# Scores of the first two attention items moved in among the value projections, in two attentions of one long fp32 kernel

## The chip, the cores and the metric
One NeuronCore of a Trainium2 chip runs the whole program in one launch. The metric is the device time of one execution in microseconds. The engines are TensorE (PE in the profile; PEld is its weight load), VectorE (DVE), ScalarE (ACT), GpSimd (POOL) and SyncE (SP), which issues the weight DMAs.

## The reference
Two transformer stacks run one after the other on 256 tokens of width 1024 and a context of 256 tokens, all in fp32. The parts that matter are the attentions of layers 0 and 1 of the first stack, which both attend densely:

```
# gqa: 16 heads of 64, 4 key/value heads; queries of x and of the context
q, k, v = split(h @ w_in); q = rms_norm(q); k = rms_norm(k); rope on the x half
p = softmax(q @ k^T * 64**-0.5); out = p @ v
# mla: 16 heads, query and key of 64 + 32 (rope), value of 64; queries of x only
q = rms_norm(cq) @ w_uq; kv = rms_norm(ckv) @ w_ukv
p = softmax((qn @ kn^T + qr @ kr^T) * 96**-0.5); out = p @ v
```

Context queries see 256 keys, x queries all 512. Feed-forward layers, other mixers (RWKV, sparse attention) and a mixture of experts follow; the change does not touch them.

## The kernel before
Each engine has its own instruction stream, written out by hand in Python; the order in the source is the order in the queue of that engine. Engines meet through named events: `did(...)` counts a semaphore up, `wait_ge(*at(...))` waits for it. The eight PSUM banks are handed out in a fixed rotation by `take`, and a taker waits for the event that frees its bank.

Weights come in 1 MB chunks through a ring of four. A matmul in fp32r with split operands needs a high and a low part of each weight unit of 1024 columns: ACT copies the high part (`hi_units`, row `WHI<-ring`), DVE subtracts for the low part (`lo_units`, row `WLO<-ring,WHI`), and PE runs three matmuls for each tile (lines 77 to 79). Scores, rope products and value products are plain fp32 matmuls of line 74, transposes are line 82, and each of them shows as two instructions. Every ACT activation is recorded at line 85.

An attention (class `Attention`) is cut into items, each a pair of heads and one or two blocks of 128 queries. Item i passes through: `scores_pe` (PE, two banks), `max_dve` (two reductions of line 105 and a small scaling), `exp_act` (ACT), `normalise_dve` (reciprocal and scalings by the row sums), `turn_pe` (eight transposes), `copy` (one bank by DVE, one by ACT) and `values_pe`. The loops `attend_pe`, `attend_act` and `attend_dve` run them in a software pipeline. In step i PE issues the scores of item i+1, the transposes of item i-1 and the value products of item i-2. ACT issues the exponentials of item i and then the copy of item i-2. GQA has 24 items, MLA 16. GQA's item 0 has two query blocks of 256 keys, items 1 and 2 have one block of 512 keys; every MLA item has one block of 512.

Before the GQA attention, `gqa_pe` projects queries and keys and last the values: four blocks t4 of 128 tokens, 24 matmuls each, with sum and rope product of query group 7 behind block 0. DVE copies each block out (`gvt`), and behind block 0 it finishes the rope of group 7 and the query scale RQ (event `rq`). Two steps of an unrelated row product (`ada_part_pe` s = 6, 7) stand between the values and the attention.

Before the MLA attention, `mla_pe` projects eight groups of keys (`mk_up`, pr = 0..7, six matmuls of 512 columns each) and then the values, for half = 0, 1 and t4 = 0..3, six matmuls each. ACT copies each key group out in two activations of 64x512 (event `mk`, pr) between its weight splits. DVE copies the shared rope part of the keys into all heads, two copies for each pr, the last with event `mkrope`. The values are copied out by DVE.

`scores_pe` first waits for the list `ready`. For GQA this is the duplicated keys (`gkd`) and the finished query group of that pair. For MLA it is one list for all pairs: `("mk", 7)`, `("mkrope",)`, `("mqr", 3)`, `("mq", 7)`, that is, the copies of the last key group, of all rope parts, and of the queries.

Of the kernel before, what the change touches and what calls it, by code (L numbers as in the profile page):

```python
# [25 lines left out]
class Signals:  # L26
# [12 lines left out]
    def did(self, name, *events):  # L39
        self.n[name] = self.n.get(name, 0) + 1  # L40
        for ev in events:
            assert ev not in self.events, ev
            self.events[ev] = (name, self.n[name])
        return self.sem(name), 1
# [8 lines left out]
    def at(self, *ev):  # L53
        if self.known is None:
            return None, 1
        return self.known[ev]
# [491 lines left out]
def program(nc, ctx, known):  # L548
# [1093 lines left out]
    def gqa_rope_pe(pe, m):  # L1642
        b = take(pe, ("gr", m), ("gsin", m))
        pe.wait_ge(*at("gqn" if m >= 8 else "gqe", m))
        pe.wait_ge(*at("d_cr", "gqa"))
        pe.mm(b[:, 0:256], gperm, g_dst(m)[:, 256:512], True, True).then_inc(*did("group", ("grot", m)))

    def gqa_pe(pe):
        st, steps = L["gqa_in"], L["ada0"]
        def second_job(k):  # L1650
            for s in {1: (0, 1, 2), 2: (3,)}.get(k, ()):
                ada_part_pe(pe, L["ada_pe"][4 + s], 1, s)
            if k == 3:
                ada_turn_pe(pe, 1)
                give(bank_of["rs", 0])

        project_block(pe, st, [(("gq", m), ("gsq", m), 512, hx(0, 512)) for m in GQA_ORDER[:4]], normed(0), second_job)
        after = [[(gqa_sum_pe, 8), (gqa_sum_pe, 9), (gqa_sum_pe, 0), (gqa_sum_pe, 1), (gqa_rope_pe, 0), (gqa_rope_pe, 1)],
                 [(gqa_spread_pe, 8), (gqa_spread_pe, 9), (gqa_sum_pe, 2), (gqa_rope_pe, 2)],
                 [(gqa_rope_pe, 8), (gqa_rope_pe, 9), (gqa_sum_pe, 3), (gqa_rope_pe, 3)],  # L1660
                 [(gqa_sum_pe, 4), (gqa_rope_pe, 4)], [(ada_turn_pe, 2), (gqa_sum_pe, 5), (gqa_rope_pe, 5)],
                 [(gqa_sum_pe, 6), (gqa_rope_pe, 6)]]
        for t, m in enumerate(GQA_ORDER[4:]):
            ada_part_pe(pe, steps[t], 2 + t // 4, t % 4)
            project_group(pe, st, 4 + t, ("gq", m), ("gsq", m), 512, hx(0, 512), normed(0))
            if t == 0:
                sums["gk"] = take(pe, ("gksum",), ("gkroot",))
                sums["gq"] = take(pe, ("gqsum",), ("rqroot",))
                keep(bank_of["gqsum",])
            for f, arg in after[t]:  # L1670
                f(pe, arg)
        pieces = [p for [(_, _, p)] in st.groups[10]]
        for t4 in range(4):
            b = take(pe, ("gv", t4), ("gvt", t4))
            for k, p in enumerate(pieces):
                pe.wait_ge(*at("lo", p.unit))
                X = HHI[:, k, 128 * t4:128 * t4 + 128], HLO[:, k, 128 * t4:128 * t4 + 128]
                m = pe.mm3(b[:, 0:256], X, split_of(p), k == 0, k == 7)
                ev = closes(p) if t4 == 3 else ()
                if k == 7:  # L1680
                    ev = ev + (("gv", t4),)
                if ev:
                    m.then_inc(*did("group", *ev))
            if t4 == 0:
                gqa_sum_pe(pe, 7)
                give(bank_of["gqsum",])
                gqa_rope_pe(pe, 7)

    def gqa_act(a):
        def out(m):  # L1690
# [44 lines left out]
    def gqa_dve(v):  # L1735
        st = L["gqa_in"]
        ropes = [[], [0, 1], [2, 8], [9, 3], [4], [5], [6]]
        lo_units(v, st.ahead[0])
        for t in range(6):
            lo_units(v, st.ahead[4 + t])  # L1740
            for m in ropes[t]:
                gqa_rope_dve(v, m)
            if t == 0:
                v.wait_ge(*at("gkroot"))
                v.recip(GK, GK).then_inc(*did("recip", ("gkrt",)))
            if t == 1:
                for m in (8, 9):
                    v.wait_ge(*at("gks", m))
                    v.wait_ge(*at("gqe", m))
                    v.tt(g_dst(m), g_dst(m), bank("gks", m)[:, :], ALU.mult).then_inc(*did("qk", ("gqn", m)))  # L1750
            if t == 5:
                ada_job_dve(v, 2)
        lo_units(v, st.ahead[10])
        for m in ropes[6]:
            gqa_rope_dve(v, m)
        for t4 in range(4):
            v.wait_ge(*at("gv", t4))
            v.cp(gVT[:, t4, :], bank("gv", t4)[:, 0:256]).then_inc(*did("v_copy", ("gvt", t4)))
            if t4 == 0:
                gqa_rope_dve(v, 7)  # L1760
                v.wait_ge(*at("rqroot"))
                v.recip(RQ, RQ).then_inc(*did("qk"))
                v.wait_ge(*last("qk"))
                v.ts(RQ, RQ, 0.125, None, ALU.mult).then_inc(*did("qk", ("rq",)))

    GQA_ROPES = (0, 1, 2, 8, 9, 3, 4, 5, 6, 7)

# [16 lines left out]
        lambda pr: [("gkd",), ("gfin", pr)], [("gvt", 3)], lambda q, hd: RQ[:, q, hd])  # L1784

    def attend_pe(pe, A, step=None):
        A.scores_pe(pe, 0)
        for i in range(A.n + 2):
            if i + 1 < A.n:
                A.scores_pe(pe, i + 1)  # L1790
            if 1 <= i <= A.n:
                A.turn_pe(pe, i - 1)
            if i >= 2:
                A.values_pe(pe, i - 2)
            if step:
                step(i)
# [10 lines left out]
                step(i)  # L1807

    def attend_dve(v, A, step=None):
        for i in range(A.n + 2):  # L1810
            if i < A.n:
                A.max_dve(v, i)
            if 1 <= i <= A.n:
                A.normalise_dve(v, i - 1)
            if i >= 2:
                A.copy(v, i - 2, 0)
            if step:
                step(i)

# [50 lines left out]
    def mla_pe(pe):  # L1870
        st = L["mla_in"]
        lat = [(("mq_in", m), ("mcq", m), 256, hx(256, 256)) for m in range(3)]
        project_block(pe, st, lat + [(("mk_in", 0), ("mck", 0), 512, hx(0, 512))], normed(2))
        project_group(pe, st, 4, ("mk_in", 1), ("mck", 1), 512, hx(0, 512), normed(2))
        for k in range(3):
            sum_pe(pe, 3, k)
        project_group(pe, st, 5, ("mk_in", 2), ("mck", 2), 512, hx(0, 512), normed(2))
        spread_pe(pe, 3)
        mla_rope_pe(pe, "k", ("mck", 2))
        for k in range(2):  # L1880
            sum_pe(pe, 4, k)

        def of_parts(parts, low):
            return (lambda k: (parts[0][:, k, :], parts[1][:, k, :])), (lambda k: [(low, k)])

        X, needs = of_parts(CQP, "cql")
        for j in range(4):
            project_group(pe, st, 6 + j, ("mr_up", j), ("mqr_raw", j), 256, X, needs)
        spread_pe(pe, 4)
        for t in range(8):  # L1890
            project_group(pe, st, 10 + t, ("mq_up", t), ("mq", t), 256, X, needs)
            if 1 <= t < 5:
                mla_rope_pe(pe, t - 1, ("mqr_raw", t - 1))
        X, needs = of_parts(CKP, "ckl")
        for pr in range(8):
            project_group(pe, st, 18 + pr, ("mk_up", pr), ("mk", pr), 512, X, needs)
        for half in range(2):
            for t4 in range(4):
                b = take(pe, ("mv", half, t4), ("mv", half, t4))
                z = slice(128 * t4, 128 * t4 + 128)  # L1900
                for k, [(_, _, p)] in enumerate(st.groups[26 + half]):
                    pe.wait_ge(*at("lo", p.unit))
                    m = pe.mm3(b[:, :], (CKP[0][:, k, z], CKP[1][:, k, z]), split_of(p), k == 0, k == 1)
                    ev = closes(p) if t4 == 3 else ()
                    if k == 1:
                        ev = ev + (("mv_up", half, t4),)
                    if ev:
                        m.then_inc(*did("group", *ev))
# [42 lines left out]
    def mla_dve(v):  # L1951
# [41 lines left out]
        v.wait_ge(*at("mqr", 3))  # L1993
        for half in range(2):
            lo_units(v, st.ahead[26 + half])
            for t4 in range(4):
                v.wait_ge(*at("mv_up", half, t4))
                v.cp(mVT[:, t4, 512 * half:512 * half + 512], bank("mv", half, t4)[:, :]).then_inc(
                    *did("v_copy", ("mv", half, t4)))
# [1774 lines left out]
    def scalar(a):  # L3774
# [19 lines left out]
        gqa_act(a)  # L3794

        def ada_rows(i):
            if i in (0, 13, 21):
                ada_row_act(a, *{0: (3, 2), 13: (6, 3), 21: (7, 6)}[i])
            if i == 18:
                hi_units(a, L["gqa_out"].first)  # L3800
        attend_act(a, gqa, ada_rows)
# [216 lines left out]
```

## Time and profile before

| | us |
|---|---|
| runs | 2056.47, 2063.47, 2063.95 |
| median | 2063.47 |
| profiled execution, span from first to last instruction | 2057.3 |
| PE busy in it | 1936.8 (94%) |
| DVE, ACT busy | 1349.8 (66%), 1073.3 (52%) |
| mean granted PE clock, share of full | 0.969 |

For the profiled execution only the span is given, no time of its own beside it. The span lies 6.2 us under the median of the runs and 0.8 us above the lowest run. GQA's value projection begins at about 120 us of the span and MLA's at 757 us.

### The profile page before, as it was taken

The numbers are of one execution on the slowest core, as the hardware profiler recorded it, in microseconds if no ns is written. First come the engines' busy times: TensorE is split into PE (matmuls) and PEld (weight loads), VectorE is DVE, ScalarE is ACT, GpSimd is POOL, SyncE is SP. The second block draws the span as 40 slices with busy tenths as digits, with TensorE's granted clock in tenths as the row PEclk, the third lists the DMA queues.
The fourth block names the chain that finished last, engine by engine and source line by source line (L and its number), as shares of the span: only waits on it lengthen the run. The fifth ranks groups of instructions, "written<-read, shape, count | busy, mean of one in ns | idle before, by whom it ended". The sixth has DMA issues, their size and how long they took to land.

```text
span 2057.3 us, 32710 instructions
## 1 busy us (share of the span) xinstructions
PE 1936.8 (94%) x13400; PEld 1652.7 (80%) x13400; DVE 1349.8 (66%) x2060; ACT 1073.3 (52%) x1744; POOL 248.5 (12%) x267
## 2 busy tenths in 40 slices
PE   5999989999999899899999889999988899999998
PEld 3775668888787785899998888999877688888886
DVE  4348546767545658678566556545665788888887
ACT  3346524333334466566555425445445577676774
POOL 1101121111100100222112412111113000000000
PEclk9999999999999999999999999999999899999999
DMA  8423343455322220245553113555542489889794
GB/s 323 161 105 123 144 175 130 169 186 180 118 80 89 91 100 22 99 169 193 213 183 130 41 43 121 199 185 205 205 164 87 188 323 344 310 330 344 307 351 162
DMA packets 52812, 364.81 MB, mean 177 GB/s; under 512 B 5936, under 2 KB 8240, under 8 KB 8880
## 3 DMA queue, kind: packets, MB, share of 16 engines
q1 hardware_dynamic: 50304, 359.68, 47.2%
q10 hardware_dynamic: 2352, 2.96, 0.5%
q8 instruction: 109, 1.79, 0.3%
q14 instruction: 47, 0.39, 0.1%
HBM read 361.57 MB, written 1.05 MB: 176 GB/s over the span
## 4 chain that ended last, share of the span: by engine, by line
PE 82%; DVE 9%; ACT 4%; issue 3%; POOL 1%; DMA 1%; SPq 0%; DVEq 0%; POOLq 0%; ACTq 0%
PE ps L77 22%; PE ps L78 21%; PE ps L79 21%; PE ps L74 15%; DVE WLO L91 2%; PE ps L82 2%; ACT R L85 2%; ACT WHI L85 1%; DVE SM L105 1%; POOL R L91 1%; DVE R L91 1%; DMA ring<-W 1%; DVE HLO L88 1%; DVE h L88 1%; DVE x L88 0%
## 5 line engine op out<-in xcount | busy, mean ns | idle before, releaser
L91 DVE TENSOR_TENSOR WLO<-ring,WHI 128x1024 fp32r<-128x1024 f32 x562 | 676.3, 1238 | 181.1 <-ACT WHI L85 180.2
L85 ACT ACTIVATE WHI<-ring 128x1024 fp32r<-128x1024 f32 x566 | 577.6, 1052 | 89.4 <-PE ps L79 85.5
L77 PE MATMUL ps<-HHI,WHI 128*128 128x256 f32 (+1 forms) x1584 | 512.9, 324 | 28.5 <-DVE HLO L88 18.6
L78 PE MATMUL ps<-HLO,WHI 128*128 128x256 f32 (+1 forms) x1648 | 524.5, 318 | 0.0
L79 PE MATMUL ps<-HHI,WLO 128*128 128x256 f32 (+1 forms) x1584 | 506.2, 320 | 0.0
L77 PEld LDWEIGHTS ps<-HHI,WHI 128*128 128x128 f32 x1584 | 303.9, 192 | 71.1 <-issue 32.0
L78 PEld LDWEIGHTS ps<-HLO,WHI 128*128 128x128 f32 x1648 | 316.0, 192 | 22.7
L79 PEld LDWEIGHTS ps<-HHI,WLO 128*128 128x128 f32 x1584 | 303.6, 192 | 23.9
L74 PE MATMUL ps<-R 64*64 64x64 f32 (+10 forms) x2448 | 192.5, 292 | 5.3 <-ACT R L85 3.2
L85 ACT ACTIVATE R<-ps,VEC 128x512 f32<-128x512 f32 (+1 forms) x106 | 69.1, 658 | 237.4 <-PE ps L79 235.6
L91 POOL TENSOR_TENSOR R<-R 128x256 f32<-128x256 f32 (+1 forms) x99 | 108.3, 1098 | 547.5 <-ACT R L85 546.3
L85 ACT ACTIVATE R<-ps 128x512 f32<-128x512 f32 (+4 forms) x234 | 109.5, 470 | 124.2 <-PE ps L74 68.4
L88 DVE SCALAR_TENSOR_TENSOR R<-ps,VEC,R 128x510 f32<-128x510 f32 (+1 forms) x176 | 107.9, 615 | 98.4 <-ACT R L85 95.2
L74 PEld LDWEIGHTS ps<-R 64*64 64x64 f32 (+5 forms) x2448 | 135.9, 153 | 45.4 <-issue 37.8
L77 PE MATMUL ps<-WHI,XSHI 128*128 128x512 f32 (+3 forms) x416 | 156.1, 375 | 3.3 <-DVE WLO L91 2.4
L78 PE MATMUL ps<-WLO,XSHI 128*128 128x512 f32 (+3 forms) x416 | 150.9, 363 | 0.0
L79 PE MATMUL ps<-WHI,XSLO 128*128 128x512 f32 (+3 forms) x416 | 150.8, 363 | 0.0
L91 POOL TENSOR_TENSOR HLO<-h,HHI 128x256 fp32r<-128x256 f32 (+1 forms) x69 | 62.3, 918 | 414.6 <-ACT HHI L85 414.6
L82 PEld LDWEIGHTS ps<-C,R 128*128 128x128 f32 x488 | 58.2, 146 | 51.1 <-issue 24.0
L77 PE MATMUL ps<-HID,WHI 128*128 128x256 f32 x352 | 98.9, 281 | 0.3 <-issue 0.2
L79 PE MATMUL ps<-HID,WLO 128*128 128x256 f32 x352 | 98.2, 279 | 0.0
L78 PE MATMUL ps<-HID,WHI 128*128 128x256 f32 x352 | 98.2, 279 | 0.0
(222 smaller groups left out, 2983.9 us busy)
## 6 DMA issues: line engine op xcount, KB each, us to landing
ring<-W SPq DMA_DIRECT2D x340, 1024.0 KB, 4.9
x<-xt SPq DMA_DIRECT2D x2, 1024.0 KB, 6.4
out<-x SPq DMA_DIRECT2D x2, 512.0 KB, 4.8
CR<-const_nsa ACTq DMA_DIRECT2D x1, 560.0 KB, 3.8
CR<-const_rw ACTq DMA_DIRECT2D x1, 448.0 KB, 3.4
CR<-const_gqa ACTq DMA_DIRECT2D x1, 320.0 KB, 9.7
CR<-const_mla ACTq DMA_DIRECT2D x1, 320.0 KB, 2.8
VEC<-vec ACTq DMA_DIRECT2D x1, 314.0 KB, 10.9
```

The source lines that it names most:

```text
L74: return self.e.matmul(out, lhsT, rhs, start=start, stop=stop)
L77: self.e.matmul(out, l[0], r[0], start=start, stop=False)
L78: self.e.matmul(out, l[0], r[1], start=False, stop=False)
L79: return self.e.matmul(out, l[1], r[0], start=False, stop=stop)
L82: return self.e.transpose(out, in_, ident)
L85: return self.e.activation(out, in_, func, **kw)
L88: return self.e.scalar_tensor_tensor(out=out, in0=in0, scalar=s, in1=in1, op0=op0, op1=op1)
L91: return self.e.tensor_tensor(out, in0, in1, op)
L105: return self.e.tensor_reduce(out, in_, AX, ALU.max, negate=negate)
```

## The change
PE: `scores_pe(0)` and `scores_pe(1)` of GQA leave `attend_pe` and stand behind value blocks t4 = 0 and t4 = 1. In MLA `scores_pe(half)` stands ahead of the four value blocks of each half. DVE: the maxima and scalings of items 0 and 1 move too. In GQA `max_dve(0)` stands behind the RQ scaling, `normalise_dve(0)` and `max_dve(1)` behind the copy of block 1, `normalise_dve(1)` behind that of block 2. In MLA `max_dve(half)` stands ahead of the value copies of the half and `normalise_dve(half)` ahead of its third copy. ACT's exponentials stay first in `attend_act`, but the row copy `ada_row_act(3, 2)` moves from behind item 0 to behind item 1. No instruction is added or removed.

```diff
@@ gqa_pe, in the loop over t4
                 gqa_rope_pe(pe, 7)
+                gqa.scores_pe(pe, 0)
+            if t4 == 1:
+                gqa.scores_pe(pe, 1)
@@ gqa_dve, in the loop over t4
                 v.ts(RQ, RQ, 0.125, None, ALU.mult).then_inc(*did("qk", ("rq",)))
+                v.wait_ge(*at("rq"))
+                gqa.max_dve(v, 0)
+            if t4 == 1:
+                gqa.normalise_dve(v, 0)
+                gqa.max_dve(v, 1)
+            if t4 == 2:
+                gqa.normalise_dve(v, 1)
@@ attend_pe
-        A.scores_pe(pe, 0)
-        for i in range(A.n + 2):
+        for i in range(1, A.n + 2):
@@ attend_dve
-        for i in range(A.n + 2):
+        for i in range(2, A.n + 2):
             if i < A.n:
                 A.max_dve(v, i)
-            if 1 <= i <= A.n:
+            if 3 <= i <= A.n:
                 A.normalise_dve(v, i - 1)
-            if i >= 2:
-                A.copy(v, i - 2, 0)
+            A.copy(v, i - 2, 0)
@@ mla_pe
         for half in range(2):
+            mla.scores_pe(pe, half)
             for t4 in range(4):
@@ mla_dve
         for half in range(2):
             lo_units(v, st.ahead[26 + half])
+        for half in range(2):
+            mla.max_dve(v, half)
             for t4 in range(4):
+                if t4 == 2:
+                    mla.normalise_dve(v, half)
@@ scalar
-            if i in (0, 13, 21):
-                ada_row_act(a, *{0: (3, 2), 13: (6, 3), 21: (7, 6)}[i])
+            if i in (1, 13, 21):
+                ada_row_act(a, *{1: (3, 2), 13: (6, 3), 21: (7, 6)}[i])
```

## Rows read from the trace of the kernel before

**Rows 1.** The page: busy time by engine, and the chain that ended last.

```profile
PE 1936.8 (94%) x13400; PEld 1652.7 (80%) x13400; DVE 1349.8 (66%) x2060; ACT 1073.3 (52%) x1744; POOL 248.5 (12%) x267
PE 82%; DVE 9%; ACT 4%; issue 3%; POOL 1%; DMA 1%; SPq 0%; DVEq 0%; POOLq 0%; ACTq 0%
```

**Rows 2.** Chain of waits around GQA's first items: start us, us, engine and line.

```profile
133.15 2.94 PE ps L74 x24
136.12 1.30 DVE SM L105 x2
137.64 2.30 ACT R L85 x8
140.18 1.15 DVE R L95 x4
...
146.20 2.08 PE ps L74 x12
...
165.40 1.64 ACT R L85 x4
```

**Rows 3.** Timeline of that stretch: start us, us, engine, operation [idle before, releaser].

```profile
124.32 0.47 PE L77 MATMUL ps<-WHI,HHI 128*128 128x256 f32 x1
124.50 1.28 ACT L85 ACT_TABLE_LOAD   x1
126.91 0.20 DVE L95 TENSOR_SCALAR RQ<-RQ 128x64 f32<-128x64 f32 x1
133.08 1.92 PE L74 MATMUL ps<-ring,SCP 128*32 128x512 f32 x16
134.93 2.85 PE L74 MATMUL ps<-R 64*128 64x256 f32 x16
141.47 1.06 PE L82 MATMUL ps<-C,R 128*128 128x128 f32 x8 [3.68 <-DVE R L95]
144.27 0.59 ACT L85 ACTIVATE R<-ps 128x512 f32<-128x512 f32 x1
```

**Rows 4.** Stretches there: length, then PE, PEld, DVE, ACT, POOL busy, clock, DMA.

```profile
137.80:141.50 3.70, 0.03 (x1) 0.07 (x2) 2.66 (x9) 3.70 (x12) 0.00 (x0) 1.00 0.82 345
142.40:145.80 3.40, 3.40 (x16) 2.52 (x15) 3.05 (x8) 2.11 (x5) 0.00 (x0) 0.50 0.00 0
146.20:150.00 3.80, 3.80 (x35) 2.35 (x36) 3.07 (x8) 2.94 (x10) 0.00 (x0) 1.00 0.00 0
```

**Rows 5.** Timeline of PE from MLA's first value matmul on.

```profile
757.63 0.40 PE L77 MATMUL ps<-WHI,CKHI 128*128 128x512 f32 x1
760.38 0.50 PE L77 MATMUL ps<-WHI,CKHI 128*128 128x512 f32 x1 [1.89 <-DVE WLO L91]
771.16 5.32 PE L74 MATMUL ps<-R 96*128 96x512 f32 x12
777.42 1.06 PE L82 MATMUL ps<-C,R 128*128 128x128 f32 x8 [0.94 <-DVE R L95]
```

**Rows 6.** Timeline of ACT and of DVE in the same stretch.

```profile
759.10 4.86 ACT L85 ACTIVATE R<-ps 64x512 f32<-64x512 f32 x8
763.86 1.05 ACT L85 ACTIVATE WHI<-ring 128x1024 fp32r<-128x1024 f32 x1
764.93 2.42 ACT L85 ACTIVATE R<-ps 64x512 f32<-64x512 f32 x4
...
766.19 1.43 DVE L99 COPY R<-R 32x512 f32<-32x512 f32 x4
```

**Rows 7.** Chain of waits where MLA's first value products begin.

```profile
781.08 2.94 PE ps L74 x20
```

**Rows 8.** Stretches in which PE resumed after an idle time, columns as above.

```profile
299.40:302.80 3.40, 3.36 (x8) 2.71 (x9) 3.33 (x8) 1.42 (x4) 0.38 (x1) 0.50 0.00 0
697.40:702.10 4.70, 4.70 (x19) 4.41 (x20) 4.63 (x9) 1.75 (x4) 1.71 (x2) 0.50 0.01 3
867.00:872.70 5.70, 5.67 (x26) 5.70 (x27) 5.63 (x12) 2.73 (x6) 3.49 (x3) 0.50 0.14 24
```

## The prediction
> **What bounds the kernel now.** I read the page first: PE is busy for 94% of the span and 82% of the chain that ended last runs over it [rows 1]. So a permutation of instructions can pay or cost only through stretches where PE stands still, and through its clock. I then read the chain of waits, the timeline and the stretches at the two places that the diff touches.
>
> In GQA, PE ends the scores of items 0, 1 and 2 at 137.8 us and then idles 3.68 us. The chain leaves PE meanwhile: DVE takes the maxima of item 0 from 136.12, ACT its exponentials from 137.64, DVE scales from 140.18, and only at 141.47 do the transposes of item 0 start [rows 2, 3]. PE was granted the full clock in the idle stretch, but about 1 us after it resumed the clock fell to 0.50, the lower level of 1.2 GHz, for 3.4 us, in which it was busy throughout; by 146.2 it is back at 1.00, 2.4 GHz [rows 4]. The first value products start at 146.20 [rows 2].
>
> In MLA, PE starts the values at 757.63, idles 1.89 us for a weight unit, starts the scores of items 0 to 2 at 771.16, and idles only 0.94 us before the transposes at 777.42 [rows 5]. ACT is the late engine here: its copies of the key groups run well behind PE and end at 764.93 + 2.42 = 767.35, and DVE's last rope copies end at 766.19 + 1.43 = 767.62 [rows 6]. That is 10 us after PE finished projecting those keys. Before, the 11.6 us of value projections covered this.
>
> **GQA, part by part.** Nothing is removed, so PE's work ahead of the first transposes is the same, and it reaches them at 141.47 - 3.68 = 137.8 us [rows 3]. Are the weights of item 0 there? Block 0's tail ends at 124.32 [rows 3]; scores 0 take about 1.1 us (the first 8 of 16 instructions in 2.85 us, the other 8 are items 1 and 2 at 0.88 each) [rows 3]. DVE is ready after the RQ scaling at 127.1, ACT after its table load at 125.8 [rows 3]. Maxima 1.3 + 0.2, exponentials 2.3 and scalings 1.3 [rows 2] end near 132.3; item 1 follows (1.5 + 1.7 + 1.1 us, copies of value blocks between them) near 136.4. Both are before 137.8, so the idle time goes entirely. The new waits on DVE hold up only the copies of value blocks 1 to 3, each for at most about 2.5 us. Nobody needs their banks so soon: seven banks rotate, and block 2's and 3's copies are used from the value products on. The row copy behind exponential 1 reads a product that ends at about 136.9, one copy of 0.6 us while ACT waits for maxima 2 anyway.
>
> What is late next is ACT's copy of item 0, which stands behind the exponentials of item 2: scores 2 end 137.8, maxima and scaling to 139.35, exponentials 1.64 to 141.0 [rows 2], copy 0.59 to 141.6 [rows 3]. PE meanwhile does transposes 0, scores 3, transposes 1, about 1.05 us each at full clock, to 140.95, and waits 0.65 us. Value products at 141.6 instead of 146.2: a gain of 4.6 us. The sum is the idle time of 3.68, plus 1.7 for the half-rate stretch of 3.4 us [rows 4], minus 0.65 for the new wait and rounding. If the clock falls anyway, 3.0 us remain; if the new wait vanishes, 5.4. I take 4.6. From 146.2 to 155.5 the old chain stays on PE, so I let the lead pass through.
>
> The lower clock after an idle stretch is told by the row. The Trainium skill (TensorE: Matmul & The Clock Gate, "What's actually happening") says that half clock is the default state and activity releases it, and that the moment at which it acts is not tied to the kernel's work, so the ramp varies from run to run. A sum without that rule would be 3.0 instead of 4.6 here, and 7.0 instead of 9.3 in the next part; the rows here agree with it.
>
> **MLA, part by part.** Now `scores_pe(0)` is ahead of the values on PE, and its list holds the last key copies and rope copies. PE's queue is in order, so all value projections wait behind it, although they need none of this. PE stands still from 757.63 to 767.67: 10.0 us. ACT's and DVE's chains do not depend on PE there; ACT works from 759.10 to 767.35 without a pause, twelve key copies at 0.6 us each and a weight split at 1.05 [rows 6]. Then the same work: values 771.16 - 757.63 - 1.89 = 11.6 us, less 0.2 for a small second wait on a weight unit that is gone too, and 5.3 us of scores 0 to 2 [rows 5]. That gives 784.4 at full clock. After long idle times PE resumed at 0.50 and stayed there for 3.4, 4.7 and 5.7 us [rows 8], half of which is lost: 1.7 to 2.9 us, I take 2.3. Transposes 0 then start at 786.7 instead of 777.42 [rows 5]: 9.3 us later. Their weights have been ready since about 777, so the 0.94 us wait is gone and already counted. Behind them the distance to the first value products is the old 3.7 us [rows 5, 7]: ACT's copy of item 0, behind exponentials 2, comes about then as well. DVE's value copies now follow PE closely and hold nobody up. Scores 1 wait for nothing new. The bank of the fifth value block is that of scores 0, freed by its exponentials some 3 us after them, while 5.5 us of values lie between. Bounds: no clock loss 7.0, the longest one 9.9.
>
> Could ACT's copies be faster while PE is silent? In the trace they take 0.59 to 0.61 us each, both while PE waited (758.5 to 760.4) and while it ran [rows 6]. The Trainium skill (PSUM — Partial Sum Buffer, "PSUM bank collisions raise a hardware error") says that the hardware does not arbitrate or stall between engines on a bank, which leaves the price as it is.
>
> No DMA is added. The weight chunks that free later (two row-product chunks in GQA by about 2 us, the value units in MLA by up to 13 us) feed stages tens of microseconds away.
>
> **Sum.** -4.6 + 9.3 = +4.7 us. The profiled execution has 2057.3 us of span, so I expect 2062.0 in its place. The three runs have a median 6.2 us above that span; on their scale it is 2063.5 + 4.7 = 2068.2. A measurement of this kernel can tell about 0.5% (10 us) from no change, so this is "the same", on the slow side.
>
> **Rivals.**
> - *Faster: MLA's scores find their keys ready.* If the list were met when PE arrives, the stall is not paid and MLA gains its 0.94 us: -4.6 - 0.9 = -5.5, 2058.0. For it: PE waits little ahead of MLA's values in the trace, so that one cannot see there how late ACT is. Against it: the end of ACT's key copies at 767.35 [rows 6]. It decides only if ACT ended them before about 762. Chance 0.06.
> - *Slower: GQA's lead is eaten, MLA's loss stays.* In the steady state values of item i wait for ACT's copy behind exponentials i+2, a loop over PE, DVE and ACT that may set the pace by itself; then the first item whose loop is late gives back the 4.6 us. +9.3, 2072.8; with the longest clock stretch 2073.4. For it: DVE and ACT are busy 3.05 and 2.11 of 3.4 us [rows 4]. Against it: the chain between 146.2 and 155.5 is PE's. Chance 0.14.
> - *The clock's phase decides.* Other idle stretches fall differently once all is shifted, and each flip of one is worth 1.7 to 2.9 us [rows 8]; two flips give 2068.2 plus or minus 4. By that page of the Trainium skill this would vary between runs. Chance 0.08.
> - *The MLA loss is absorbed later* by a wait that keeps its own time, such as a weight transfer: -4.6, 2058.9. The chain has 1% of DMA [rows 1]. Chance 0.04.
>
> **How the numbers follow.** The forecast has 0.68. Its own range is +1.6 (7.0 - 5.4) to +6.9 (9.9 - 3.0). With the runs' own spread of 7 us below the median, and the slow rival above, the range is 2057 to 2075. Slower by over 0.5% needs +10.3, which only the slow rival or bad clock phases plus scatter reach: 0.12. Faster by over 0.5% needs everything to go well and more: 0.04. Within: 0.84.
>
> **What would show it.** In the profile after: PE idle under 1 us before GQA's first transposes and clock 1.00 from there to the first value products, about 4.6 us earlier against the start of the values. In MLA, a wait of 10 us of a PE matmul of line 74 (96x512) for ACT or DVE, then a stretch at 0.50, and the first transposes about 29 us after the end of the key projections instead of 19.8. I am wrong if that wait is short, or if the GQA attention ends no earlier.

## The result, and the profile after

| | before | after |
|---|---|---|
| median of 7 runs each, us | 2063.07 | 2069.46 |
| lowest and highest | 2056.47, 2063.95 | 2066.46, 2070.43 |
| span of the profiled execution | 2057.3 | 2066.6 |

The ratio after to before is 1.0035, with a 95% interval of [1.0022, 1.0048]: 7.2 us slower, between 4.5 and 9.9. The forecast was +4.7 us and 2068.2 us.

The page hardly differs from that of before [rows 1]: the same count of instructions, PE busy at 94% again, and the same shares in the chain that ended last.

```profile
PE 1941.4 (94%) x13400; PEld 1654.4 (80%) x13400; DVE 1350.1 (65%) x2060; ACT 1075.6 (52%) x1744; POOL 248.1 (12%) x267
PE 82%; DVE 9%; ACT 4%; issue 3%; POOL 1%; DMA 1%; SPq 0%; DVEq 0%; POOLq 0%; ACTq 0%
```

**GQA.** First the chain of waits (start us, us, engine and line), which answers to [rows 2].

```profile
135.64 2.94 PE ps L74 x20
138.60 1.30 DVE SM L105 x2
...
140.12 2.12 ACT R L85 x5
...
142.38 2.14 PE ps L74 x12
```

The chain leaves PE once, as before, but PE is busy beside it. The timeline (start us, us, operation, [idle before, releaser]) has the transposes of items 0 and 1 in the place of the old idle time [rows 3]:

```profile
137.43 1.13 PE L74 MATMUL ps<-R 64*128 64x512 f32 x4
...
138.49 1.09 PE L82 MATMUL ps<-C,R 128*128 128x128 f32 x8
...
140.57 1.09 PE L82 MATMUL ps<-C,R 128*128 128x128 f32 x8
...
142.38 2.14 PE L74 MATMUL ps<-R 128*64 128x256 f32 x12 [0.71 <-ACT R L85]
```

The 3.68 us of idle time are gone, and 0.71 us of waiting for ACT's copy of item 0 has come. ACT's row copy, which the change moved behind exponential 1, starts at 137.56 us, with ACT waiting 2.00 us before it and 1.97 us behind it. In the stretches (length; PE, PEld, DVE, ACT, POOL busy; clock; DMA) the half rate of [rows 4] is gone too:

```profile
136.40:140.50 4.10, 4.10 (x32) 1.98 (x24) 2.48 (x6) 0.97 (x2) 0.00 (x0) 1.00 0.63 232
140.50:142.30 1.80, 1.17 (x10) 0.86 (x8) 1.73 (x6) 1.80 (x6) 0.00 (x0) 1.00 1.01 419
142.40:146.00 3.60, 3.60 (x30) 2.20 (x32) 2.76 (x7) 2.59 (x9) 0.00 (x0) 1.00 0.24 102
```

**MLA.** PE's timeline shows the last matmul of the key projections, the stall, and the items behind it. It answers to [rows 5].

```profile
754.97 0.40 PE L79 MATMUL ps<-CKHI,WLO 128*128 128x512 f32 x1
...
765.43 3.75 PE L74 MATMUL ps<-R 96*128 96x512 f32 x4 [10.07 <-DVE R L99]
774.88 1.88 PE L74 MATMUL ps<-R 96*128 96x512 f32 x4
782.10 1.88 PE L74 MATMUL ps<-R 96*128 96x512 f32 x4
783.82 1.04 PE L82 MATMUL ps<-C,R 128*128 128x128 f32 x8
...
787.62 3.01 PE L74 MATMUL ps<-R 128*64 128x128 f32 x20 [0.17 <-ACT R L85]
```

Scores 0 take 3.75 us where scores 1 and 2 take 1.88: they ran at half clock. Transposes 0 start 28.6 us after the end of the key projections (754.97 + 0.23 to 783.82), against 19.8 before. What PE waits for is the work of ACT and DVE, unchanged from [rows 6] but for 2.3 us of shift (PE's key projections end 2.4 us earlier than before). DVE's last low part waits 1.80 us for ACT's high part, and the last rope copies stand behind it:

```profile
762.60 2.42 ACT L85 ACTIVATE R<-ps 64x512 f32<-64x512 f32 x4
...
762.61 1.23 DVE L91 TENSOR_TENSOR WLO<-ring,WHI 128x1024 fp32r<-128x1024 f32 x1 [1.80 <-ACT WHI L85]
763.86 1.42 DVE L99 COPY R<-R 32x512 f32<-32x512 f32 x4
```

And the stretches, of the stall, of what follows, and one at 728.7 that before has not:

```profile
755.60:765.40 9.80, 0.00 (x0) 0.00 (x0) 6.64 (x14) 9.54 (x16) 0.00 (x0) 0.69 0.34 114
765.40:770.60 5.20, 5.17 (x10) 2.87 (x11) 1.29 (x2) 0.92 (x1) 0.00 (x0) 0.59 0.47 192
770.60:783.80 13.20, 13.20 (x52) 9.41 (x51) 8.78 (x18) 2.89 (x8) 0.00 (x0) 1.00 0.00 0
...
728.70:732.10 3.40, 3.40 (x18) 3.40 (x17) 2.10 (x4) 1.58 (x3) 0.00 (x0) 0.50 0.00 0
```

**Where the 9.3 us of the two spans lie.** The table gives, for one and the same ACT activation in each profiled execution, its start less its start before (activations counted from the beginning up to 757, from the end after it). The columns besides "after" are kernels of the experiments below. The three with "share" leave out some of ACT's copies from 755.5 us on, so their row 757 takes the last activation ahead of these, at 755.2.

```
us of before   after   GQA   MLA    pair   late   share  late+  share
                       alone alone  ready         4      share3 3
 102           +0.18  -0.29  -0.33  +1.49  -0.35  +0.01  +1.54  +1.54
 146           -4.09  -4.55  -0.33  -2.78  -4.62  -4.26  -2.73  -2.73
 285           -3.74  -4.19  -0.31  -2.42  -4.25  -3.91  -2.39  -2.37
 690           -4.09  -4.01  -0.38  -0.69  -4.06  -4.23  -0.68  -0.68
 757           -2.32  -4.18  -0.34  +1.47  -4.25  -2.42  +1.47  +1.52
 801           +6.62  -2.96  +9.38  +2.12  -3.46  -2.92  -0.11  -0.31
 990           +6.39  +0.70  +7.12  +2.14  -3.55  -3.55  -0.87  -0.53
1401           +9.47  +3.77  +6.56  +5.43  -4.78  -4.37  -1.81  -1.95
2047           +9.31  +6.68  +6.55  +5.23  -3.77  -0.90  -0.18  -0.66
```

For after, GQA gives -3.9 (102 to 285) and MLA +8.9 (757 to 801), together +5.0. The rest lies where the code is the same in both: +1.8 between 690 and 757 (the stretch at 728.7) and +3.3 between 1300 and 1400. So a single pair of profiles shows here 4 us that the edit did not make, and only the table by place tells them apart.

### The profile page after: what moved, and what is told of

The parts are those of the page before. It is cut to its first block, busy times and chain, and to the rows that moved or that the text cites. A ratio compares the mean times of both kernels' runs of the same rounds, so it can differ in the third digit from the quotient of the medians.

```text
span 2066.6 us, 32711 instructions
## 1 busy us (share of the span) xinstructions
PE 1941.4 (94%) x13400; PEld 1654.4 (80%) x13400; DVE 1350.1 (65%) x2060; ACT 1075.6 (52%) x1744; POOL 248.1 (12%) x267
## 4 chain that ended last, share of the span: by engine, by line
PE 82%; DVE 9%; ACT 4%; issue 3%; POOL 1%; DMA 1%; SPq 0%; DVEq 0%; POOLq 0%; ACTq 0%
PE ps L77 22%; PE ps L79 21%; PE ps L78 21%; PE ps L74 15%; DVE WLO L91 2%; ACT R L85 2%; PE ps L82 2%; ACT WHI L85 1%; DVE SM L105 1%; POOL R L91 1%; DVE R L91 1%; DMA ring<-W 1%; DVE HLO L88 1%; DVE h L88 1%; DVE x L88 0%
## 5 line engine op out<-in xcount | busy, mean ns | idle before, releaser
L77 PEld LDWEIGHTS ps<-WHI,XSHI 128*128 128x128 f32 x416 | 78.3, 188 | 22.8 <-DVE WLO L91 11.5
```

What stands on the lines that cost most here:

```text
L77: self.e.matmul(out, l[0], r[0], start=start, stop=False)
```

## The experiments

The columns of a row are as above. Each time stands beside runs of the kernel before on the same chip.

### One half of the change at a time

```diff
# gqa_only: mla as before            # mla_only: gqa as before
-    mla.scores_pe(pe, half)         -    gqa.scores_pe(pe, 0), (pe, 1)
-    mla.max_dve / normalise_dve     -    gqa.max_dve / normalise_dve
+    attend_pe(pe, mla, None, 0)     +    attend_pe(pe, gqa, vector_steps, 0)
```

> The change in GQA alone (with the row copy's move); MLA as before. My theory: PE's idle stretch of 3.7 us ahead of the first transposes and the half clock behind it go, the first value products come 4 to 4.6 us earlier after the start of the value projection, and the whole is 4 to 5 us faster than before (ratio 0.998). Rival, the lead is eaten in the steady state of the attention: the start is earlier, but the attention ends as before, ratio 1.000.

> The change in MLA alone; GQA as before. My theory: PE waits 10 us for the rope and key copies ahead of the scores of item 0, the first transposes start about 28.5 us after the end of the key projections instead of 19.8, and the whole is 8 to 10 us slower than before (ratio 1.004 to 1.005). Rival, the 6 us between the two kernels come from elsewhere (clock phases after MLA): ratio under 1.002.

GQA alone: 2060.88 us (12 runs) against 2065.54 (32), ratio 0.9985 [0.9969, 1.0001]. MLA alone: 2073.44 us (9 runs), ratio 1.0056 [1.0037, 1.0075]. The two ratios add up to +0.41%, where after has +0.35%. So the signs are those of the prediction, though by the runs alone GQA's gain is not clear of noise: its interval just reaches 1. In places, GQA alone gains 3.9 us by 285 and keeps it to 757; MLA alone loses 9.7. PE in the MLA of the second kernel:

```profile
767.42 3.75 PE L74 MATMUL ps<-R 96*128 96x512 f32 x4 [9.99 <-DVE R L99]
```

GQA alone then loses 1.2 us in an MLA that is as before. Its wait for a weight unit is the old one of 1.89 us [rows 5], but the matmuls behind it ran at half clock (0.52 from 756.5 to 760.0), and there was no such stretch before:

```profile
756.21 0.59 PE L77 MATMUL ps<-WHI,CKHI 128*128 128x512 f32 x1 [1.91 <-DVE WLO L91]
```

### MLA: is it the list of keys, and is it the place?

```diff
# pair_ready: the list asks for what this pair needs, not for the last
-    lambda pr: [("mk", 7), ("mkrope",), ("mqr", 3), ("mq", 7)]
+    lambda pr: [("mk", pr), ("mkrope", pr), ("mqr", pr // 2), ("mq", pr)]
# late: the old list; scores 0 and 1 among the values of the second half
-            mla.scores_pe(pe, half)
             for t4 in range(4): ...
+                if half and t4 < 2:
+                    mla.scores_pe(pe, t4)
```

> The changed kernel, but MLA's scores of a pair wait for the key, rope and query copies of that pair alone. If the list that all pairs share is the cause, the wait of 10 us ahead of scores 0 goes. What is late next is DVE, whose maxima of item 0 stand behind all rope copies: the bank that block 0 of half 1 takes over from scores 0 is freed by its exponentials, so PE should wait about 2.7 us there. First transposes 19.5 us after the end of the key projections, the whole about 4 to 5 us faster than before and 10 us faster than the changed kernel. Rival, the wait is for ACT's last key copies in any case: the 10 us stay.

> The changed kernel, but MLA's scores 0 and 1 stand behind value blocks 0 and 1 of half 1, when the copies are done; maxima and scalings follow on DVE. If the place decides, PE waits under 0.2 us for the list, the first transposes start 18.9 us after the end of the key projections (19.8 before), and the whole is 5 to 6 us faster than before. Rival, scores among values cost something by themselves: slower than the kernel with GQA's part alone.

Pair ready: 2062.78 us (12 runs), ratio 0.9982 [0.9962, 1.0001]. Late: 2063.35 us (12 runs), ratio 0.9992 [0.9973, 1.0011]. Both take the loss of MLA away: +0.65 and +0.79 us from 757 to 801 instead of +8.9. The first transposes start 19.7 and 20.0 us after the end of the key projections (expected 19.5 and 18.9). In the first, PE's stall of 10 us falls apart into short waits for ACT, of which four are shown; the wait of 2.7 us for a bank behind DVE, which I had expected, did not come:

```profile
759.56 1.95 PE L74 MATMUL ps<-R 96*128 96x512 f32 x4 [0.30 <-ACT R L85]
...
761.82 0.50 PE L77 MATMUL ps<-WHI,CKHI 128*128 128x512 f32 x1 [0.30 <-ACT R L85]
...
768.97 1.96 PE L74 MATMUL ps<-R 96*128 96x512 f32 x4 [1.37 <-ACT R L85]
...
783.13 3.01 PE L74 MATMUL ps<-R 128*64 128x128 f32 x20 [0.66 <-ACT R L85]
```

It is the wait for the last of the keys that costs, and not moving the scores as such. But neither place gains over before: there PE idled only 0.94 us ahead of the transposes, and now ACT's copies end the waits. In late PE does not stop for the list, but it has the same wait of 1.90 us for a weight unit, with half clock behind it, as GQA alone, which loses 1.2 us in the same place. Against that kernel the late place is worth 0.4 us.

### What the clock costs behind each idle time

Both kernels keep PE busy in the idle time with matmuls of the identity that no output uses; they are extra work.

```diff
# mla_filled, of after: ahead of scores 0 in MLA
+    for _ in range(28):
+        pe.mm(bs[0][:, 0:384], ident, C0[:, 0:384], True, True)
# gap_filled, of before: the same, 10 times, ahead of GQA's transposes 0
```

> The changed kernel with 28 extra fp32 matmuls of 128x384 on constants (about 9 us of PE work) put ahead of MLA's wait for the key copies, into the bank that scores 0 then overwrite. If PE's idle time lowers the clock, as I think, the granted clock stays at 1.00, scores 0 take 1.9 us instead of 3.75, and the first transposes start 2 us earlier after the end of the key projections (26.4 instead of 28.4). Rival, the 3.75 us are slow for another reason: they stay.

> The kernel before with 10 extra matmuls of the same kind (about 3.2 us) in PE's idle time ahead of GQA's first transposes, into the bank that the transposes then overwrite. By my theory the clock does not fall, scores 3 and transposes 1 take 1.05 us each instead of 2.0 and 1.7, and the first value products come 1.4 to 1.7 us earlier, though the wait itself stays. That sizes the clock's share of GQA's 4.3 us. Rival: no change of the clock, nothing gained.

They took 2078.18 and 2068.84 us, one run each. I had mis-sized the fill: each of these plain fp32 matmuls is two instructions of 0.33 us, not one, so it overran the wait in both and the time as a whole says nothing. The places behind it can still be read:

```profile
755.59 18.30 PE L74 MATMUL ps<-C 128*128 128x384 f32 x56 [0.34 <-ACT R L85]
773.72 1.88 PE L74 MATMUL ps<-R 96*128 96x512 f32 x4
...
789.98 1.04 PE L82 MATMUL ps<-C,R 128*128 128x128 f32 x8
```

Scores 0 take 1.88 us and from their start to the transposes are 16.26 us, against 18.39 in after: the clock's part of the MLA loss is 2.1 us. After, MLA alone and after share all have the stall and 3.75 us for scores 0. In GQA, filled:

```profile
137.74 6.72 PE L74 MATMUL ps<-C 128*128 128x384 f32 x20
144.29 1.04 PE L82 MATMUL ps<-C,R 128*128 128x128 f32 x8
...
147.69 2.14 PE L74 MATMUL ps<-R 128*64 128x256 f32 x12 [0.27 <-ACT R L85]
```

Transposes 0 to the first value products take 3.40 us with a wait of 0.27, against 4.66 us before (141.47 to 146.13 in the same view; the chain in [rows 2] has 146.20): 1.3 to 1.5 us are the clock's.

### The row copy's move

```diff
# row_at_0, of after: ACT's row copy stays behind exponential 0
-            if i in (1, 13, 21):
+            if i in (0, 13, 21):
```

> The changed kernel with the row copy of ACT back behind item 0. It reads a product that ends 13 us after scores 0, and exponentials 1 then stand behind it. I expect exponentials 1 at about 138 instead of 133.9 us, maxima 2 behind scalings 1 on DVE 2.4 us later, and the first value products 2.4 us later, or 4.1 if PE's wait of 3 us lowers the clock. Rival, the move is worth nothing: first value products as in the changed kernel.

2069.63 us, one run. The whole gain of GQA is gone: an activation that starts at 157.8 us before starts 0.40 us later here, and this execution was 0.48 us late at 102 us already. PE, from the transposes of item 1 on:

```profile
141.47 1.09 PE L82 MATMUL ps<-C,R 128*128 128x128 f32 x8
145.10 2.75 PE L74 MATMUL ps<-R 128*64 128x256 f32 x12 [2.54 <-ACT R L85]
147.78 1.97 PE L82 MATMUL ps<-C,R 128*128 128x128 f32 x8
```

and ACT:

```profile
137.86 0.60 ACT L85 ACTIVATE R<-ps 128x512 f32<-128x512 f32 x1 [6.44 <-PE ps L74]
138.35 0.77 ACT L85 ACTIVATE R<-ps,SM,RQ 128x512 f32<-128x512 f32 x1
```

ACT stands 6.44 us in front of the row copy, whose product comes behind the values, with exponential 1 queued behind it. Item 1's scaling and item 2's maxima follow late, the copy of item 0 with them, PE waits 2.54 us instead of 0.71, and transposes 2 then take 1.97 us instead of 1.09, at half clock. The first value products come 2.4 us later than in after, once the 0.3 us are taken off by which this execution was behind that one at 102 us: the 2.4 expected. This line of the diff, one 0.6 us copy, decides over the whole gain in GQA: with it left in place, moving the scores brings nothing.

### Taking ACT's lateness away

```diff
# DVE takes the first copy of key groups pr < N
             a.wait_ge(*at("mk_up", pr))
-            a.act(mK[0:64, 2 * pr, :], bank("mk_up", pr)[0:64, :], ACT.Copy)
+            if pr < N:
+                a.wait_ge(*at("mkd", pr))
+            else:
+                a.act(mK[0:64, 2 * pr, :], bank("mk_up", pr)[0:64, :], ACT.Copy)
# share: gqa_only, N = 4; share_three: gqa_only, N = 3
# late_share: late, N = 3; after_share: after, N = 3
```

> GQA's part alone, and in MLA DVE takes the first copy of the key groups 0 to 3 from ACT, the late engine. ACT saves 2.4 us up to its last weight splits, so PE's wait of 1.9 us for a weight unit should fall to about 0.7 and the small one behind it go: the MLA part 1.4 us shorter than in the kernel with GQA's part alone, 3 us where that one's clock fell at this wait. Rival, DVE becomes late and the wait stays.

> GQA as changed; MLA's scores 0 and 1 stand behind the first two value blocks of the second half, as in the kernel 'late', and DVE instead of ACT takes the first copy of key groups 0 to 2, so that ACT's run of weight splits ahead of the values ends earlier. Theory (ACT's lateness sets what is left in MLA): the wait for the first weight unit of the values, 1.90 us in 'late', falls under 0.7 us and no stretch at half clock follows it; from the end of the key projections to the first transposes about 18.3 us instead of 19.97, so MLA gains 1 to 2 us against before, GQA gains 3.9; together about -5.5 us, ratio 0.9973. Rival (DVE becomes the late engine there, since it takes three copies more and has the low parts to make): the wait only changes its releaser's queue and stays near 1.9 us, MLA +0.8 as in 'late', total -3.1, ratio 0.9985. The scatter of the runs is about 2 us on a median of 12, so the landmarks of the profile decide between the two.

> The changed kernel, with one edit: DVE instead of ACT takes the first copy of key groups 0 to 2. Three copies of 0.6 us leave ACT. Theory (PE's 10 us of standing still is the lateness of ACT's key copies behind PE): the stall falls by the 1.8 us taken from ACT or somewhat less, to 8.0 to 8.8 us. Rival (DVE's rope copies, which the profile names as releaser, set it by themselves): it stays at 10 us or grows, since DVE has 1 to 2 us more to do ahead of them.

> GQA alone as changed, MLA as before, and DVE instead of ACT takes the first copy of key groups 0 to 2 (0 to 3 in the earlier kernel 'share'). Theory (ACT then waits less for DVE at group 3, where it stood 2.35 us): the two waits for weight units, 0.42 and 1.04 us there, become at most one short one; end of key projections to first transposes 18.8 instead of 19.3; total -4.5 to -5.0 us against before, ratio 0.9977. Rival (ACT and DVE are equally loaded there, so a copy only changes hands): 19.3 again, total -4.3. If 'late_share' is not faster than this one, the late place of MLA's scores brings nothing.

| | us, runs | before | ratio | MLA, 757 to 801 |
|---|---|---|---|---|
| share | 2059.34 (12) | 2064.63 (17) | 0.9974 [0.9961, 0.9987] | -0.50 |
| late share | 2056.48 (12) | 2061.39 (23) | 0.9982 [0.9964, 1.0000] | -1.58 |
| share three | 2059.03 (12) | 2061.39 (23) | 0.9991 [0.9976, 1.0007] | -1.83 |
| after share | 2067.67 (1) | 2061.39 (23) | | +7.3 |

In after with three copies taken from ACT, the stall falls by 2.3 us to 7.8 (8.0 to 8.8 expected), though DVE, the engine that the profile names, got more to do:

```profile
767.05 3.75 PE L74 MATMUL ps<-R 96*128 96x512 f32 x4 [7.77 <-DVE R L99]
```

So ACT's chain sets the stall, and DVE's rope copies only come last in it, behind a low part that waits for ACT's high part. In share three and in late share the wait of 1.9 us for the weight unit falls to 0.4, and no half-clock stretch follows. First share three, then late share:

```profile
760.42 0.50 PE L77 MATMUL ps<-WHI,CKHI 128*128 128x512 f32 x1 [0.43 <-DVE WLO L91]
...
777.10 1.06 PE L82 MATMUL ps<-C,R 128*128 128x128 f32 x8 [0.94 <-DVE R L95]
...
780.69 3.01 PE L74 MATMUL ps<-R 128*64 128x128 f32 x20
```

```profile
760.37 0.50 PE L77 MATMUL ps<-WHI,CKHI 128*128 128x512 f32 x1 [0.42 <-DVE WLO L91]
...
776.40 1.04 PE L82 MATMUL ps<-C,R 128*128 128x128 f32 x8
...
780.90 3.01 PE L74 MATMUL ps<-R 128*64 128x128 f32 x20 [0.86 <-ACT R L85]
```

With the scores at the late place the transposes come 0.7 us earlier, and the value products 0.2 us later: the lead ends at ACT's copy of item 0. What MLA's half of the change could bring at best is thus 0.94 us of idle time, and that wait changes its name when it is won. Nobody needs the scores earlier there. The share of ACT's copies is what brings MLA 1.8 us.

From the end of the key projections to the first transposes it is 18.0 us in share three and 17.3 in late share, both less than expected (18.8 and 18.3). In share it is 19.3: ACT stood 2.35 us for DVE's copy of group 3, and PE waited 0.42 us for the first weight unit and 1.04 us for the second. Against GQA alone, whose clock fell at its wait, share's MLA part is 1.7 us shorter, where I had expected 3.

The totals of late share and share three do not show the -5.5 and the -4.5 to -5.0 us expected (ratios 0.9973 and 0.9977). In the profiled execution of each, 3.9 us are lost between 285 and 757, in code that no edit touched. Whether their other runs lose them too was not seen, so this explains the totals only in part at best. Only share has an interval wholly under 1, against before (-5.4 us, between 2.7 and 8.1). Share three has a better place table in MLA and a worse ratio, so which of the three is the fastest is not settled by these runs. All three intervals lie under the lower end of after's.

## Why the prediction was right

1. *GQA, -4.6 (bounds -5.4 to -3.0).* The value products start at 142.38 instead of 146.20, with the stage itself beginning 0.18 us later, so 4.0 us earlier, and 3.9 from there to the end of the attention. The step for the idle time of 3.68 and the one for the new wait (0.65, measured 0.71) held. The clock's term of 1.7 was mis-sized a little: the filled kernel has 1.3 to 1.5. The transposes start at 138.49, 0.5 us behind my 137.8 and that shift, so PE's work ahead of them is not "the same". Scores of items 1 and 2 by themselves take 1.06 us each, where I had read 0.88 in a run of three, and the matmuls on either side of scores start 0.2 to 0.3 us apart instead of 0.12; against this, the last two value blocks run at a shorter cadence (below). These 0.5 us and the clock's term are what is missing from 4.6.
2. *The row copy.* I gave its move one clause, as harmless. It is harmless, but had the copy stayed, that would have cost about 4 us. The prediction didn't see that the gain hangs on it.
3. *MLA, +9.3 (bounds +7.0 to +9.9).* Stall 10.0, measured 10.07; clock 2.3, measured 2.1; transposes "about 29 us after the end of the key projections", measured 28.6. Together +8.9, and +9.7 with MLA alone. That ACT's and DVE's chains do not depend on PE there held, and that ACT sets the time was shown by the kernel that takes copies from it.
4. *The old distance of 3.7 us to the first value products* held: 783.82 to 787.62 is 3.8.
5. *Sum.* +4.7 forecast, +5.0 measured at the two places, +7.2 [4.5, 9.9] by the runs. The forecast lies in that interval near its lower end.
6. *The rivals.* MLA's scores did not find their keys ready. The steady state of GQA ate 0.3 of the 4.3 us by which it led at 146 (measured from 102), not all: the rival was named rightly as possible, its price was small. The MLA loss was absorbed nowhere. The clock's phase had a part, +1.8 us at 728.7 in the profiled execution of after, within the two flips of 1.7 to 2.9 that I had allowed. The larger scatter, the matmul cadence told below, the prediction did not have.

What stays open is the 2 us between +5.0 by place and the +7.2 of the medians; the interval holds both, and the scatter below is of that size.

## What to carry to other kernels

- Before a step is moved ahead of independent work in an in-order queue, read when the last thing that it waits for is done, on the slowest engine of that chain, and not where the present wait ends. Here the idle time to be won was 0.94 us, and the late engine ran 10 us behind PE.
- If a wait list asks for the last of many parts, move the work late or split the list. Here both took the 9 us back. To gain more, unload the engine that is late.
- A neighbour in another engine's queue can hold the whole gain: look through each queue for what stands in front of the instruction that is to run earlier, and ask when its own input comes.

## What the runs showed of the hardware

**A matmul cadence with two values.** In feed-forward stages in which PE never waits, the same matmuls start every 0.113 us in one execution and every 0.117 to 0.118 in another, for the whole stage. Before, then after, first and last row of 12 and of 11 steps:

```profile
1349.73 0.28 PE L79 MATMUL ps<-HHI,WLO 128*128 128x256 f32 x1
...
1351.09 0.28 PE L79 MATMUL ps<-HHI,WLO 128*128 128x256 f32 x1
```

```profile
1355.83 0.28 PE L77 MATMUL ps<-HHI,WHI 128*128 128x256 f32 x1
...
1357.12 0.28 PE L79 MATMUL ps<-HHI,WLO 128*128 128x256 f32 x1
```

The groups by line over this stage, 1312 to 1390 of before and 1318 to 1397 of after, have mean durations of 277 and 281 ns. Each such stage costs 3.3 to 3.9 us more. It happened in after, GQA alone and pair ready at 1300 to 1400, and in GQA alone at 880 to 990 as well, and not in before, MLA alone or late. There it does not go with the edit: row at 0 and after share contain both halves too and had the short cadence. In GQA it does. In all ten profiled kernels in which scores 1 stand behind value block 1, the 48 value matmuls behind them start every 0.113 us; in before, MLA alone and gap filled they start every 0.118. That is 0.2 us of GQA's gain. What sets the cadence I don't know. The Trainium skill (TensorE: Matmul & The Clock Gate, "Wait — 56ns, not 53.3ns?") gives one value for back-to-back matmuls at full clock, the columns divided by 2.4 GHz plus about 2.5 ns. For 256 columns that would be 109 ns, an estimate from its formula; the runs show 113 and 117.

**Half-clock stretches that one execution has and another has not.** The profiled executions of pair ready, late share and share three were 1.5 us late already at 102 us, ahead of every edit, and all three ran at half clock at 731 us, where before did not. Before, then share three:

```profile
731.00:734.40 3.40, 3.40 (x31) 3.40 (x32) 2.36 (x5) 2.43 (x6) 0.73 (x1) 1.00 0.01 2
```

```profile
731.00:734.40 3.40, 3.40 (x19) 3.40 (x20) 2.30 (x5) 1.59 (x3) 0.73 (x1) 0.58 0.01 2
```

PE was busy throughout in both, and its last idle time, 0.39 us, lay 2.3 us ahead of the window in share three. Another such stretch at 622 us comes right behind a wait of 2.01 us; before has the same wait at 624.3 us, and the clock stays full. With the two stretches these three lose 1.7 us from 285 to 690 and 2.2 us from 690 to 757, 3.9 in all, the size of the whole gain in GQA. Up to there they differ from GQA alone and late in nothing but those 1.5 us, and these two lose nothing. Being late at 102 us is not needed for the second stretch, though: after and share have it too (from 728.7 and 728.5 us), with a loss of 1.8 us from 690 to 757, and they were at most 0.2 us late there. The cause stays open. Cadence and clock may be much of the scatter of one kernel, which ran, before, from 2056.37 to 2073.85 us over 32 runs; it was profiled once, so this was not shown. An edit worth 4 us is seen in a profile by place; in the total even a dozen runs leave it at the edge of the noise.
